# GLA head with tokens as rows and its gate projection inside; modulation matmuls on column groups, spread over heads and first FFN

## What is computed

```python
def gla_chunked(q, k, v, log_a, s0):
    ...
    b = jnp.cumsum(log_a.reshape(B, H, N, C, dk), axis=3)
    ...
    q_dec = q * jnp.exp(b)
    k_inv = k * jnp.exp(-b)
    k_to_end = k * jnp.exp(b_last - b)
    ...
    att = jnp.where(mask, jnp.einsum('bhnik,bhnjk->bhnij', q_dec, k_inv), 0.0)
    o_intra = jnp.einsum('bhnij,bhnjv->bhniv', att, v)
    u = jnp.einsum('bhnck,bhncv->bhnkv', k_to_end, v)
    ...
    def step(s, inp):
        d, uu = inp
        return d[..., None] * s + uu, s
    s_final, s_prev = lax.scan(step, s0, (jnp.moveaxis(decay, 2, 0), jnp.moveaxis(u, 2, 0)))
    ...
    o_inter = jnp.einsum('bhnck,bhnkv->bhncv', q_dec, s_prev)

def finish(o, g, h):
    Bh, H, L, dv = o.shape
    o = rmsnorm(o, hn_g).transpose(0, 2, 1, 3).reshape(Bh, L, H * dv)
    return ((o * jax.nn.silu(g.astype(f32))) @ w_out).astype(h.dtype)
```

## Time and profile before

| | us |
|---|---|
| median of 3 runs | 1914.05 (1911.96 to 1921.38) |
| profiled execution | 1914.71 |
| its span (first to last instruction) | 1913.0 |
| PE busy | 1802.5 (94%) |
| POOL, DVE, ACT busy | 621.6, 617.4, 532.5 (28 to 32%) |
| mean granted clock | 0.972 |

### The profile page before, as it was taken

One profiled execution on the slowest core, in us unless ns is written; L12 is line 12 of the kernel. 1 busy time (PEld: TensorE's weight loads), 2 busy tenths in 40 slices (PEclk: granted clock), 3 DMA queues, 4 the chain that ended last, 5 costly groups with the idle time before them and its releaser, 6 DMA issues.

```text
span 1913.0 us, 24968 instructions
## 1 busy us (share of the span) xinstructions
PE 1802.5 (94%) x10172; PEld 1489.6 (78%) x10172; DVE 617.4 (32%) x693; ACT 532.5 (28%) x531; POOL 621.6 (32%) x449
## 2 busy tenths in 40 slices
PE   7899999989998999999999998997877999999997
PEld 2588787877787888888888886776765778888886
DVE  2743323343435121111211133665556322112022
ACT  2422122323323211111111122367545232112122
POOL 1220202102241343233432352353425434545443
PEclk9899999999999999999999999998988999999999
DMA  7312304122223112222122114112243433233221
GB/s 269 89 57 77 110 23 131 40 81 88 77 66 110 51 59 66 66 66 66 45 65 66 55 55 143 34 45 66 66 132 110 122 98 104 94 95 102 88 94 72
DMA packets 197444, 159.87 MB, mean 84 GB/s; under 512 B 7202, under 2 KB 193940, under 8 KB 197396
## 3 DMA queue, kind: packets, MB, share of 16 engines
q1 hardware_dynamic: 197396, 159.20, 26.7%
HBM read 157.08 MB, written 2.10 MB: 83 GB/s over the span
## 4 chain that ended last, share of the span: by engine, by line
issue 51%; PE 28%; POOL 15%; DVE 3%; DMA 1%; ACT 1%; POOLq 0%; DVEq 0%; ACTq 0%
POOL w_lo L466 14%; PE duo L522 9%; PE duo L525 9%; PE duo L528 9%; PE mod_psum L558 2%; DMA mod_ring<-in_w_mod_dram 1%; DVE gates_r L1512 1%; DVE scan_h L1523 1%; DVE scan_h L1506 1%; DVE u_conv L1473 0%; DVE scan_h L1517 0%; DVE y_rows L1545 0%; DVE scan_h L1525 0%; ACT u_hi L1081 0%; PE duo L823 0%
## 5 line engine op out<-in xcount | busy, mean ns | idle before, releaser
L466 POOL TENSOR_TENSOR w_lo<-raw,w_hi 128x512 fp32r<-128x512 f32 (+1 forms) x420 | 600.5, 1461 | 1264.2 <-ACT w_hi L840 1264.2
L522 PE MATMUL duo<-a_hi,w_hi 128*128 128x512 f32 (+1 forms) x1712 | 513.1, 358 | 20.2 <-DVE a_lo L1245 8.9
L528 PE MATMUL duo<-a_hi,w_lo 128*128 128x512 f32 (+1 forms) x1712 | 511.6, 357 | 0.0
L525 PE MATMUL duo<-a_lo,w_hi 128*128 128x512 f32 (+1 forms) x1712 | 507.5, 355 | 0.0
L840 ACT ACTIVATE w_hi<-raw 128x2048 fp32r<-128x2048 f32 (+1 forms) x105 | 193.7, 1849 | 563.5 <-PE duo L528 563.5
L522 PEld LDWEIGHTS duo<-a_hi,w_hi 128*128 128x128 f32 x1712 | 283.5, 191 | 79.7 <-issue 21.0
L525 PEld LDWEIGHTS duo<-a_lo,w_hi 128*128 128x128 f32 x1712 | 280.7, 190 | 47.8
L528 PEld LDWEIGHTS duo<-a_hi,w_lo 128*128 128x128 f32 x1712 | 281.6, 190 | 46.1
L1434 DVE TENSOR_TENSOR hid<-duo,gate 128x1024 f32<-128x1024 f32 (+1 forms) x33 | 33.5, 1044 | 502.2 <-PE duo L528 502.2
L558 PE MATMUL mod_psum<-mod_ring,cs 128*2 128x128 f32 x1280 | 166.0, 290 | 29.0 <-DMA mod_ring<-in_w_mod_dram 28.9
L558 PEld LDWEIGHTS mod_psum<-mod_ring,cs 128*2 128x2 f32 x1280 | 109.3, 89 | 81.0 <-DMA mod_ring<-in_w_mod_dram 36.3
(11 more groups left out here) (190 smaller groups left out, 1568.6 us busy)
## 6 DMA issues: line engine op xcount, KB each, us to landing
raw<-in_ffn_w_dram SPq DMA_DIRECT2D x120, 512.0 KB, 4.3
mod_ring<-in_w_mod_dram SPq DMA_DIRECT2D x80, 512.0 KB, 4.0
raw<-in_gla_w_in_dram SPq DMA_DIRECT2D x24, 512.0 KB, 5.7
mod_first<-in_w_mod_dram SPq DMA_DIRECT2D x8, 1024.0 KB, 15.8
raw<-in_lru_w_in_dram SPq DMA_DIRECT2D x16, 512.0 KB, 4.5
raw<-in_ffn_w_dram SPq DMA_DIRECT2D x16, 384.0 KB, 3.6
raw<-in_gla_w_out_dram SPq DMA_DIRECT2D x8, 512.0 KB, 4.9
raw<-in_lru_w_out_dram SPq DMA_DIRECT2D x8, 512.0 KB, 6.5
```

Source lines behind the costliest of these rows:

```text
L466: pool.tensor_tensor(w_lo[b][:, k:k + 2, 0:cols], raw[b][:, k:k + 2, 0:cols], w_hi[b][:, k:k + 2, 0:cols].bitcast(F32), ALU.subtract).then ...
L522: pe.matmul(tile_out(ps, t, part, n), wh, act_hi[:, k, s:s + n], start=begin, stop=False, skip_group_check=True)
L525: pe.matmul(tile_out(ps, t, part, n), wh, act_lo[:, k, s:s + n], start=False, stop=False, skip_group_check=True)
L528: mm = pe.matmul(tile_out(ps, t, part, n), wl, act_hi[:, k, s:s + n], start=False, stop=last, skip_group_check=True)
```

## The change

1. Tables. `duo_table` and `chunk_table` give every PSUM use and every weight chunk a name, buffer and count; all loops are written out. PE's program grows from 3244 to 7883 rows.
2. Modulation matmuls. `cs` becomes 128 x 8 x 32, zero but for two columns. The matmul of k goes to column group k mod 4 of the array, so four partial sums stand on partitions 0, 32, 64 and 96 of `mod_psum`. The row copy takes 128 partitions; `turn` multiplies with `pick`, which adds the four.
3. Order of the pieces. They go in slots of two: four slots in a head, and one slot after each of the 22 w1 and w3 tiles of the first FFN; sections 6's first four go singly after the tiles of `project_out(0)`. Turns of sections 6 to 11 stand after w1 tiles. The norms, the LRU and the second FFN hold none.
4. Output of a head. Tokens are rows: 6 matmuls of scores by 256 values, 22 of q (64 tokens) by a state (256 values), in column group 0 or 64 for even and odd chunks. ACT squares with a sum along the row and takes the scale as Exp(-0.5 Ln), DVE multiplies once (`o_rows`), PE transposes back (`o_turns`, 12), DVE multiplies with silu(g) and the norm's weight (`o_columns`). This comes one head later. `rms_sum`, the reciprocal and the gate stage are gone.
5. Gate projection. The chunk of g is multiplied inside the head, two of its eight rows ahead of each group of state matmuls. The states of a group are written in the order 4, 0, 2, 1, 3, 5; numbers 4 and 5 share a bank and join by a semaphore, `fifth_state`. ACT changes its table between silu and log/exp in every head.

```diff
+                for k in range(KT):
+                    g = 32 * (k % 4)
+                    mm = pe.matmul(mod_psum[g:g + 32, at_:at_ + P], cs[:, k], mod_ring[p % 2][:, k], start=k < 4,
+                                   stop=k >= 4, tile_position=(0, g), skip_group_check=True)
...
+            def state_matmuls(h, g):
...
+                for s in (4, 0, 2, 1, 3, 5)[:len(chunks)]:
...
+                    if s == 5:
+                        pe.wait_ge(fifth_state, 2 * h + g // 2 + 1)
...
+            def o_matmuls(h):
+
+
+                q = ("o", h)
+                pe.wait_ge(att_ready, h + 1)
+                wait_moved(pe, ("u", h, 3))
+                duo_wait(q)
+                for tau in range(TT):
+                    pe.matmul(flat(q)[:, tau * 256:(tau + 1) * 256], att[:, tau], v_tok[:, tau], start=tau % 2 == 0,
+                              stop=False, skip_group_check=True)
+                for tau in range(TT):
+                    for d in range(2):
+                        for c in range(2):
+                            n = 2 * tau + c
+                            s = STATE_BEFORE[d][n]
+                            if s is not None:
+                                mm = pe.matmul(flat(q)[CHUNK * c:CHUNK * (c + 1), tau * 256:(tau + 1) * 256],
+                                               q_dec[:, d, n * CHUNK:(n + 1) * CHUNK], states[:, s], start=False,
+                                               stop=d == 1, tile_position=(0, CHUNK * c), skip_group_check=True)
...
+            for h in range(HEADS):
+                s = SEC_HEAD + h
+                gate_matmuls(h)
+                if h:
+                    o_matmuls(h - 1)
+                    mod_slot((s - 1, 6), (s - 1, 7))
+                tile_pair(("qk", h), ("qk", h), BOTH, a_hi, a_lo)
+                if h:
+                    turn(s - 1, 1)
+                v_matmuls(h)
+                mod_slot((s, 0), (s, 1))
+                k_turns(h)
+                if h:
+                    o_turns(h - 1)
+                mod_slot((s, 2), (s, 3))
+                att_matmuls(h)
+                chunk_wait(("g", h))
+                duo_wait(("g", h))
+                for g in range(4):
+                    mm = tile_rows(("g", h), ("g", h), BOTH, a_hi, a_lo, (2 * g, 2 * g + 1))
...
+                    state_matmuls(h, g)
+                turn(s, 0)
+                mod_slot((s, 4), (s, 5))
+            o_matmuls(HEADS - 1)
+            mod_slot((5, 6), (5, 7))
...
+                        tile_rows(name, name, parts, a_hi, a_lo, range(6), ready=ready)
+                        o_turns(HEADS - 1)
+                        done(tile_rows(name, name, parts, a_hi, a_lo, (6, 7), ready=ready))
...
             def o_scales(h):
+                for tau in range(TT):
+                    steps.mark(act.activation(o_tok[:, tau], flat(("o", h))[:, tau * 256:(tau + 1) * 256], ACT.Square,
+                                              accum_out=o_rms[:, 0, tau:tau + 1]))
```

More of the change, by code:

```diff
@@ L407, in _ @@
-            ffn_loads(0, 7)
+            g_load(0)
+            for h in range(HEADS):
+                s = SEC_HEAD + h
+                if h < HEADS - 1:
+                    wait_done(sp, ("gate", h))
+                    gate2_load(h + 1)
+                    qk_load(h + 1)
+                else:
+                    columns(("out", 0, 0), gla_w_out[0], 0)
+                mod_pieces(s, 0, 1)
+                if h < HEADS - 1:
+                    v_load(h + 1)
+                else:
+                    columns(("out", 0, 1), gla_w_out[0], 256)
+                mod_pieces(s, 2, 3)
+                if h < HEADS - 1:
+                    g_load(h + 1)
+                mod_pieces(s, 4, 5, 6, 7)
@@ L427, in _ @@
-            for n in range(2, 4):
-                columns(C_OUT1 + n, lru_w_out[0], 256 * n)
-            ffn_loads(1, 11)
+                    r = raw[CH[("lg", n, d)] % 2]
+                    load(("lg", n, d), (r[:, 0:2], ga[d, n]), (r[:, 2:4], gx[d, n]))
+            for n in range(4):
+                columns(("out", 1, n), lru_w_out[0], 256 * n)
+            ffn_loads(1)
             sp.wait_ge(mod_used, 2 + 8 * 10)
@@ L483, in _, with duo_wait @@
                                    ALU.subtract).then_inc(early_split, 1)
-            with pool.Fori(0, (CHUNKS - C_OUT1 - 2) // 2) as i:
-                for b in range(2):
-                    low((C_OUT1 + 2 + b, 2, i))
+            for ch in range(CH[("out", 1, 2)], len(CH)):
+                low(ch)
         @block.tensor
         def _(pe):
-            def duo_wait(q):
-                if isinstance(q, tuple) or q >= 2:
-                    pe.wait_ge(duo_moved[par(q)], half(q))
-            def chunk_wait(ch):
-                pe.wait_ge(hi_ready, whole(ch) + 1)
-                pe.wait_ge(lo_ready, 4 * (whole(ch) + 1))
+            def duo_wait(name):
+                slot, use, _ = DUO[name]
+                if use:
+                    pe.wait_ge(duo_moved[slot], use)
@@ new lines, in tile_row @@
+            def tile_row(chunk, name, parts, act_hi, act_lo, rows, k, t, k0=0, begin=None):
+                ps, hi, lo = duo(name), w_hi[CH[chunk] % 2], w_lo[CH[chunk] % 2]
+                last = k == rows - 1
+                wh, wl = hi[:, k0 + k, t * P:(t + 1) * P], lo[:, k0 + k, t * P:(t + 1) * P]
+                for part, s, n in parts:
+                    opens = k == 0 and (begin is None or begin or part == 0)
+                    pe.matmul(tile_out(ps, t, part, n), wh, act_hi[:, k, s:s + n], start=opens, stop=False,
+                              skip_group_check=True)
+                for part, s, n in parts:
+                    pe.matmul(tile_out(ps, t, part, n), wh, act_lo[:, k, s:s + n], start=False, stop=False,
+                              skip_group_check=True)
+                for part, s, n in parts:
+                    mm = pe.matmul(tile_out(ps, t, part, n), wl, act_hi[:, k, s:s + n], start=False, stop=last,
+                                   skip_group_check=True)
+                return mm
@@ L571, in turn @@
                 mm.then_inc(mod_turned, 1)
[L573 to L579 removed]
             def token_sums(n, parts):
[L583 removed]
+                q = ("stat", n)
                 pe.wait_ge(summed, SUMMED[n])
@@ new lines, in ffn, with norm_sums @@
+                    for i in range(4):
+                        name = ("w2", layer, part, i)
+                        hb = HID[layer][part]
+                        rd = (lambda k: pe.wait_ge(hid_ready, hb + k // 2 + 1) if k % 2 == 0 else None)
+                        tile_pair(name, name, parts, h_hi, h_lo, rows=n, ready=rd if i == 0 else None)
+                        if layer == 0 and part == len(FFN_PARTS) - 1 and i == 0:
+                            turn(11, 1)
+            def norm_sums(n, parts):
```

1095 lines of the change are left out of this document (504 added, 591 removed).

## The result

The changed kernel takes 1846.46 us (median of 4, 1843.58 to 1848.63) against 1917.72 for the kernel before (median of 4, 1911.96 to 1923.16): ratio 0.963, 95% interval 0.959 to 0.966. That is 71 us less, where 86 were forecast. The profiled execution has a span of 1843.2.

What follows compares the result with a forecast made beforehand. PE, busy 94% of the span, was taken as the bound. Terms -2.8 - 101.6 + 6.8 - 5.2 + 37.1 - 8.3 - 8.6 - 3.4 = -86.0 against the profiled 1914.7 gave 1828.7, forecast 1829 us, range 1812 to 1850.

Steps and rivals of the forecast that it cites:

- Unit prices: Modulation slots, head outputs, turns: four column groups run side by side; piece 0.43 us, slot 1.15, output 7.7, turn 0.98.
- Step 1: Start of the kernel: matmuls of sections 0 and 1 get faster, -2.8 us (between -4 and -1).
- Steps 4 and 6: Norms before first FFN, LRU and second FFN: without modulation pieces they end earlier, -5.2, -8.3 and -8.6 us.
- Step 7: LRU and last projection: no row copy ahead of rounding u, 4.6 us earlier, less 1.2 for lost cover: -3.4.
- Step 8: Whole kernel: loops written out, tables and the row copy on 128 partitions change nothing, 0 us.
- Step 2: Heads and gate stage: shorter pieces and outputs, state wait covered by g rows; 429.3 to 327.7 us, -101.6.
- Step 3: Output projection: 4.6 us uncovered chain behind the last head, plus a turn and four single pieces: +6.8 (3 to 10).
- Step 5: First FFN: nothing waits inside its tiles, so 22 slots and 12 turns are paid in full, +37.1 us.
- R2: Column groups and states: program order lets only two passes overlap; slot 2.0 us, total 1861, 1877 with states; chance 0.25.
- R3: Column groups: no overlap over columns, slots 3.7 + 0.1 us, outputs 12.4; total 1943, slower; chance 0.12.
- R4: Heads: new waits, a late ACT link or the ring, 5 to 8 us in each head; total 1850 to 1860; chance 0.13.

## Why the prediction was right, and where its sum was off

The direction, the mechanism and the range held; the sum lacked 15 us of loss (71 measured, 86 forecast, both against their own times before). Heads and output projection alone lacked 20 us; 3.8 came back in the other stretches.

- *Unit prices*: right. Slot 1.02 for 1.15, output of a head 7.68 for 7.7, turn 0.88 for 0.98. The guess from two row groups to four column groups held.
- *Step 1, start*: -3.4 for -2.8. *Steps 4 and 6, norms*: -6.1, -8.7, -10.1 for -5.2, -8.3, -8.6. *Step 7*: -2.2 for -3.4. *Step 8, loops written out*: no gap at the old loop ends; 0 held.
- *Step 2, heads*: the term that was mis-sized. Its parts: the waits for pieces 2 and 3 were 7.9 in the sum (3.1 in head 0, 1.6 in the others) and 11.1 in the trace (both loads start together, and the second lands after 6.3 us, later than the 4.0 of the earlier trace rows); the lower clock behind that wait, about 1.0 a head in the scores, had no term, though the earlier trace rows showed its like (a piece of 3.54 instead of 1.91 behind a wait, 1.6 us, which the sum took as 1.4); the states were taken at their old price, and their new order cost 1.3 a head. 3.2 + 4.0 + 5.2 is 12.4 of the 13.6 missed; 1.2 stay open. Moving the slot gave 14.8, the order 4.3 to 5.2. What was right is that the rows of g cover the state scan: no wait for it is left in the list.
- *Step 3, output projection*: +13.2 for +6.8. The chain behind the last transposes was priced about rightly (4.1 us of wait for 4.6); the low clock behind it (eight pairs of matmuls 0.64 us apart instead of 0.35, 2.3 us) had no term, and the buffer that two uses share was not looked at (5.0 us by the run that gave tile 1 the other buffer). The order of buffer uses can be followed in the table of part 1 of the change.
- *Step 5, FFN*: +35.8 for +37.1. With a slot two tiles start 18.17 us apart, 18.95 with a turn.
- *R2* fell for column groups (order inside a piece does nothing) and stood in part for the states and for eleven products in a row. The Trainium skill ("TensorE: Matmul & The Clock Gate", section "Part 3: Packing small matmuls — row/col tiling") gives 3.07 times for four row tiles. Here, on four column groups, a slot went from 3.58 to 1.02, 3.5 times. The same section of the Trainium skill states that matmuls keep program order in start and end. The pieces in their other order don't bear that out (1.05 us for 1.01); only the eleven products in a row came near to what it would cost (8.8 us for 9.4).
- *R3* (no overlap over columns) fell. Its total looks right for the run with one group (less the 19 us for the outputs, which kept their groups there, its sum is 1924, and that run took 1929), but by luck: it adds 95 us to a base of 1829, where 83 us came on top of 1846.
- *R4* happened in part: what could be won back in a head was 3.7 us instead of 5 to 8, by the ring and the clock; no wait for a buffer that ACT moves was in the list.

## What to carry to other kernels

Work that is made shorter gives nothing where it stood in someone else's wait: column groups alone gave this kernel nothing (0.4% slower), and were worth 4% (1929 against 1846 us) once 44 of the 80 pieces had moved to where PE is never waiting. A sum over PE should carry a term for the clock behind each wait of a few microseconds, and each use of a PSUM buffer that is put in or taken out changes who waits for whom one use later. The cheapest places for filler work are the long waits for other engines, and there too the ring that feeds it sets how much goes in.

## What the runs showed of the hardware

Matmuls on four column groups of 32 run side by side at full rate: 32 passes of 128 fp32 columns in 1.02 us, against 0.108 a pass alone. In the run with the pieces four times over, 64 passes took 1.89 us (224.57 to 226.46), so 32 more cost 0.87, a quarter of 32 x 0.108. The order among them matters little within the eight matmuls of a piece and much with eleven of a group in a row, on groups of 64 (8.8 us for 4.9).

The granted clock was at its lower level (1.2 GHz) behind waits of about 1 to 4 us for a DMA or DVE (0.9 and 2.1 us ahead of the scores in head 1, 4.1 us in the output projection). With column groups alone it stayed there for 21 us (0.50 from 236.3 to 257.5) in which small matmuls kept PE busy (64 columns for 128 by 128 weights); with longer work in the place of the wait it was at the higher level (2.4 GHz, 1.00 from 236.3 to 248.4).

The large tiles have two paces. In the stretch from 640 to 1160 us, inside the first FFN in both, the kernel before executed 2946 records and the one with column groups alone 3001, at a granted clock of 1.00:

```profile
640.00:1160.00 520.00, 520.00 (x2946) 450.86 (x2945) 93.44 (x95) 83.68 (x58) 189.06 (x128) 1.00 0.20 63
```

```profile
640.00:1160.00 520.00, 520.00 (x3001) 454.54 (x3001) 88.52 (x89) 84.84 (x60) 188.66 (x128) 1.00 0.19 61
```

A chunk takes 16.96 us at one pace and 16.64 at the other (twelve chunks from 741.64 to 945.16 us, and from 761.16 to 960.84), 10 us over that FFN, with the same instructions. The runs of the kernel with column groups alone fall into two clusters, 1917 to 1922 and 1929 to 1932 us, which would fit; at the slower pace its profiled run would have had a span of 1927, 14 above the kernel before. What chooses the pace stays open.
